# Decoder step: order of the operand splits at the entry of the gate-up product, a room of its own for one quarter, and the gate rows' loads on another queue

## The reference

```python
xp = xp + g1 * mix_out(o, bg * cy, attn_out_g[l], conv_out_g[l], w_o[l])        # output projection, residual
xp = xp + g2 * swiglu(modulate(xp, ln2_g[l], sh2, sc2), w_gu[l], w_down[l])     # the same for xs, with its own gates

def modulate(x, g, shift, scale):
    return rmsnorm(x, g) * (1.0 + scale) + shift

def swiglu(h, w_gu, w_down):
    g, u = jnp.split(h @ w_gu, 2, axis=-1)
    return (jax.nn.silu(g) * u) @ w_down
```

## Time and profile before

| | us |
|---|---|
| median of 3 runs | 961.69 (961.57 to 964.09) |
| profiled execution | 954.09 |
| its span, first to last instruction | 952.3 |
| TensorE busy | 911.9 |
| VectorE busy | 636.5 |
| ScalarE busy | 406.6 |
| GpSimd busy | 294.8 |

### The profile page before, as it was taken

How to read it: one execution, slowest core, us unless ns; L and a number is a source line. 1 busy time by engine, 2 the same in 40 slices (tenths; PEclk the granted TensorE clock), 3 DMA queues, 4 the chain that set the end, 5 groups by cost and what they waited for, 6 DMA issues and landing times.

```text
span 952.3 us, 16418 instructions
## 1 busy us (share of the span) xinstructions
PE 911.9 (96%) x6253; PEld 761.1 (80%) x6253; DVE 636.5 (67%) x1238; ACT 406.6 (43%) x818; POOL 294.8 (31%) x289
## 2 busy tenths in 40 slices
PE   6999999999999999899999988989999999999997
PEld 5777888999985557666644578989999999888886
DVE  3565773698646777667433879999998888544444
ACT  3674552221344335766601654444444445333220
POOL 4111000000132441534300347867767774000000
PEclk9999999999999999999999999999999999999999
DMA  8998313264449885473104232533333333522101
GB/s 274 397 393 294 106 50 97 81 208 150 148 140 350 321 320 190 130 257 89 35 1 132 85 104 64 148 89 89 90 89 90 105 110 107 200 89 89 72 1 50
DMA packets 84075, 138.83 MB, mean 146 GB/s; under 512 B 4259, under 2 KB 55027, under 8 KB 79646
## 3 DMA queue, kind: packets, MB, share of 16 engines
q1 hardware_dynamic: 74146, 95.47, 30.7%
q0 software_dynamic: 9568, 42.18, 12.5%
q10 hardware_dynamic: 284, 0.13, 0.0%
HBM read 130.58 MB, written 11.31 MB: 149 GB/s over the span
## 4 chain that ended last, share of the span: by engine, by line
PE 77%; DVE 9%; DMA 5%; issue 3%; ACT 3%; POOL 2%; SPq 0%; DVEq 0%; ACTq 0%; POOLq 0%
PE bank L2299 16%; PE bank L2301 16%; PE bank L2300 16%; PE bank L2293 6%; PE bank L2379 3%; PE bank L2813 3%; PE bank L2823 3%; DMA wring<-in_w_ada 2%; PE bank L2660 2%; PE bank L2630 2%; PE bank L2328 2%; PE bank L2793 2%; DMA arena<-in_cache_k_slc,idh 2%; PE bank L2309 2%; PE bank L2308 2%
## 5 line engine op out<-in xcount | busy, mean ns | idle before, releaser
L2299 PE MATMUL bank<-s,ring_hi 128*128 128x288 f32 x620 | 185.9, 300 | 10.5 <-DVE s L521 7.1
L2300 PE MATMUL bank<-s,ring_lo 128*128 128x288 f32 x620 | 184.5, 298 | 0.0
L2301 PE MATMUL bank<-s,ring_hi 128*128 128x288 f32 x620 | 183.8, 296 | 0.0
L2299 PEld LDWEIGHTS bank<-s,ring_hi 128*128 128x128 f32 x620 | 117.7, 190 | 11.5 <-DVE s L521 7.6
L2301 PEld LDWEIGHTS bank<-s,ring_hi 128*128 128x128 f32 x620 | 118.2, 191 | 0.0
L2300 PEld LDWEIGHTS bank<-s,ring_lo 128*128 128x128 f32 x620 | 117.8, 190 | 0.0
L521 DVE TENSOR_TENSOR ring_lo<-mem,ring_hi 128x512 fp32r<-128x512 f32 x84 | 107.6, 1300 | 0.0
L2293 PE MATMUL bank<-cst,arena 128*128 128x128 f32 (+1 forms) x538 | 69.1, 280 | 10.1 <-DMA arena<-in_cache_k_cmp,idx 6.5
L2293 PEld LDWEIGHTS bank<-cst,arena 128*128 128x128 f32 (+1 forms) x538 | 59.5, 143 | 23.8 <-issue 15.5
L886 POOL DMA_INDIRECT arena<-in_cache_k_slc,idh x16 | 15.4, 964 | 171.3 <-PE bank L2301 165.7
L521 DVE TENSOR_TENSOR dn_w<-wring,dn_w 128x2048 fp32r<-128x2048 f32 (+1 forms) x11 | 23.1, 2096 | 65.8 <-ACT dn_w L518 65.8
(11 more groups left out here) (363 smaller groups left out, 2099.0 us busy)
## 6 DMA issues: line engine op xcount, KB each, us to landing
wring<-in_w_gu SPq DMA_DIRECT2D x44, 512.0 KB, 5.1
wring<-in_w_ada SPq DMA_DIRECT2D x16, 1024.0 KB, 12.6
wring<-in_w_in SPq DMA_DIRECT2D x10, 1024.0 KB, 5.0
wring<-in_w_down SPq DMA_DIRECT2D x10, 1024.0 KB, 5.0
wring<-in_w_ada SPq DMA_DIRECT2D x16, 512.0 KB, 8.9
proj<-in_x_prompt SPq DMA_DIRECT2D x4, 512.0 KB, 12.2
mem<-in_state_k_win POOLq DMA_DIRECT2D x8, 256.0 KB, 8.6
mem<-in_state_v_win POOLq DMA_DIRECT2D x8, 256.0 KB, 6.0
```

The lines of the kernel that those rows point to most:

```text
L2299: pe.matmul(dst, sh, ml, start=first and k == 0, stop=False)
L2300: pe.matmul(dst, sl, mh, start=False, stop=False)
L2301: ins = pe.matmul(dst, sh, mh, start=False, stop=last and k == len(pairs) - 1)
```

## The change

Five edits, all around the entry of the gate-up product.

1. DVE does the last tile's modulation (L2168, L2170 before) right behind the low parts of (1,4) and slot 5. The low parts (0,7), (1,8) and (0,6), which stood ahead of it, come later: (1,8) right behind it, (0,7) ahead of (1,7), (0,6) ahead of (1,6). (2,8) and (2,4) come ahead of the first sum of the last segment. `SEG_LOW`, `SEG_HIGH` and ACT's list are put in that order.
2. POOL's `sums(1)` waits for the low part (2,4).
3. Operand 8 gets rooms of its own (`units[8]`): the high part in `arena`, where tiles 0 and 1 of the residual stood, the low part in `uvT`, which the output projection reads until its end. So ACT waits with (0,8) until the stores of those two tiles have landed (`x1_first_out`), and DVE does the low part of (0,8) behind the last of the projection.
4. Operand 3 then no longer waits for `plain_step(3)` on ACT. Its three high parts move ahead of slots 8 to 11 and its three low parts ahead of slot 9, from a place ahead of slot 12.
5. The four loads of the gate rows move from POOL's product loop to SP, behind the last tile's store, with a semaphore of their own.

```diff
-        units[8] = units[3]
+        units[8] = (arena, 2 * 1024), (uvT, 4 * HALF)
@@ sp
             x1_store(4)
+            sp.wait_ge(x1_ready, 10)
+            for y in range(2):
+                at0, cols = (2 + y) * 32 * 512, slice(512 * y, 512 * y + 512)
+                sp.dma_start(gbc[:, 0, cols], bass.AP(g_rows.tensor, at0, [[0, 128], [1, 512]])).then_inc(gates_back, 16)
+                sp.dma_start(gbc[0:TS, 1, cols], bass.AP(g_rows.tensor, at0 + 512, [[512, NB], [0, NQ], [1, 512]])
+                             ).then_inc(gates_back, 16)
             for i in range(g0 + 4, d0 + 4):
                 load(i)
@@ pool
             sums(0)
+            pool.wait_ge(seg_low, SEG_LOW.index((2, 4)) + 1)
             sums(1)
...
-                if p == 24:
-                    pool.wait_ge(x1_ready, 10)
-                    gates_load(1)
@@ act
-                if m == 3:
-                    want_filled(act, ("gp", 3))
...
                 if t == 3:
+                    act.wait_ge(x1_first_out, 32)
                     sums_high(0, 8)
...
             plain_silu(0, c11s[0])
-            sums_high(1, 5)
             sums_high(2, 8)
             sums_high(2, 4)
             slot_cast(6)
+            first_copy(1)
+            sums_high(1, 5)
             sums_high(1, 7)
-            first_copy(1)
...
             plain_silu(2, c21)
+            for s in range(3):
+                sums_high(s, 3)
             slot_cast(8)
             slot_cast(9)
             first_copy(2)
             slot_cast(10)
             slot_cast(11)
-            for s in range(3):
-                sums_high(s, 3)
@@ dve
+                    if n and t == 5:
+                        sums_low(0, 8)
...
                             sums_low(0, 4)
-                            sums_low(0, 8)
                             slot_rest(4)
...
             slot_rest(5)
-            sums_low(0, 7)
-            sums_low(1, 8)
-            sums_low(0, 6)
             key = ("hT", 4, 0)
...
-            dve.tensor_tensor(s_raw[5][:, :, seg], a21, a22, ALU.add).then_inc(seg_last, 1)
+            sums_low(1, 8)
             sums_low(2, 8)
             sums_low(2, 4)
+            dve.tensor_tensor(s_raw[5][:, :, seg], a21, a22, ALU.add).then_inc(seg_last, 1)
...
+            sums_low(0, 7)
             sums_low(1, 7)
...
             sums_low(2, 7)
-            sums_low(1, 6)
-            sums_low(2, 6)
+            for s in range(3):
+                sums_low(s, 6)
             slot_rest(8)
+            for s in range(3):
+                sums_low(s, 3)
             plain_product(3, c21, actT[:, 0, HALF:TOK])
...
             slot_rest(11)
-            for s in range(3):
-                sums_low(s, 3)
             slot_rest(12)
```

More of the change, by code:

```diff
@@ L74 @@
 SEGS = ((2, 0, 96), (3, 96, 224), (4, 224, 288))
-SEG_HIGH = [(0, 4), (0, 8), (0, 5), (0, 7), (0, 6), (1, 4), (1, 8), (1, 5), (2, 8), (2, 4), (1, 7), (2, 5), (1, 6), (2, 7), (2, 6),
+SEG_HIGH = [(0, 4), (0, 8), (0, 5), (0, 7), (0, 6), (1, 4), (1, 8), (2, 8), (2, 4), (1, 5), (1, 7), (2, 5), (1, 6), (2, 7), (2, 6),
             (0, 3), (1, 3), (2, 3)]
-SEG_LOW = [(0, 4), (0, 8), (0, 5), (1, 4), (0, 7), (1, 8), (0, 6), (2, 8), (2, 4), (1, 5), (1, 7), (2, 5), (2, 7), (1, 6), (2, 6),
+SEG_LOW = [(0, 4), (0, 5), (0, 8), (1, 4), (1, 8), (2, 8), (2, 4), (1, 5), (0, 7), (1, 7), (2, 5), (2, 7), (0, 6), (1, 6), (2, 6),
            (0, 3), (1, 3), (2, 3)]
@@ L441, in decoder_kernel @@
         win_loaded = [sem(f"win_loaded{i}") for i in range(2)]
-        gates_out, gates_in = sem("gates_out"), sem("gates_in")
+        gates_out, gates_in, gates_back = sem("gates_out"), sem("gates_in"), sem("gates_back")
         xin_loaded, rows_back, rows_out, stored, kvc_stored = (
             sem(n) for n in ("xin_loaded", "rows_back", "rows_out", "stored", "kvc_stored"))
-        x1_out, x1_back, slot_high, slot_low, made, seg_sum, seg_last, seg_high, seg_low, first_silu, second_silu, t_made, c22_made, gu_done = (
-            sem(n) for n in ("x1_out", "x1_back", "slot_high", "slot_low", "made", "seg_sum", "seg_last", "seg_high", "seg_low",
+        x1_out, x1_first_out, x1_back, slot_high, slot_low, made, seg_sum, seg_last, seg_high, seg_low, first_silu, second_silu, t_made, c22_made, gu_done = (
+            sem(n) for n in ("x1_out", "x1_first_out", "x1_back", "slot_high", "slot_low", "made", "seg_sum", "seg_last", "seg_high", "seg_low",
                              "first_silu", "second_silu", "t_made", "c22_made", "gu_done"))
@@ L818, in x1_store @@
                 sp.wait_ge(x1_ready, 5 + t + 1)
-                sp.dma_start(x1_rows[128 * t:128 * t + TM[t], :], xin[t][0:TM[t], :]).then_inc(x1_out, 16)
+                sp.dma_start(x1_rows[128 * t:128 * t + TM[t], :], xin[t][0:TM[t], :]).then_inc(x1_first_out if t < 2 else x1_out, 16)
             for i in range(done + 14, g0 + 2):
@@ L827, in _ @@
             x1_store(4)
+            sp.wait_ge(x1_ready, 10)
[4 more added lines that the diff above has]
+                             ).then_inc(gates_back, 16)
             for i in range(g0 + 4, d0 + 4):
                 load(i)
-            sp.wait_ge(x1_out, 80)
+            sp.wait_ge(x1_first_out, 32)
+            sp.wait_ge(x1_out, 48)
             want_filled(sp, ("gu",) + FAST[-1])
@@ L1423, in _ @@
             slot_cast(6)
+            first_copy(1)
+            sums_high(1, 5)
             sums_high(1, 7)
-            first_copy(1)
             sums_high(2, 5)
+            slot_cast(7)
             sums_high(1, 6)
-            slot_cast(7)
             sums_high(2, 7)
@@ L2248, in _ @@
                     if f == 3:
-                        dve.wait_ge(x1_out, 80)
+                        dve.wait_ge(x1_first_out, 32)
+                        dve.wait_ge(x1_out, 48)
                     dve.tensor_tensor(actT[:, f, 0:HALF], c11s[f % 3], t_sum, ALU.mult).then_inc(gu_done, 1)
@@ L2259, in _ @@
                 low_job(j)
-            dve.wait_ge(gates_in, 128)
+            dve.wait_ge(gates_back, 64)
             dve.wait_ge(x1_back, 80)
```

## The result

The changed kernel takes 955.21 us (median of 7 runs, 950.59 to 957.63), the kernel before 961.76 (7 runs). The ratio is 0.9924, 95% interval 0.9896 to 0.9953: faster by 0.76%. The forecast was 959.5, no change that a measurement can tell. Its range held the time, but the likeliest case, no change, was the wrong one.

The account below looks back on a forecast made before the run. TensorE, busy 911.9 of 952.3 us, bounds the kernel; only about 13.2 us of stalls and clock drops can return. Entry +0.4 and gate rows -2.6 sum to -2.2: 959.5 us, own range 957.5 to 961.5, wider range 954.5 to 963.5.

Parts of the forecast that it names:

- The first stall: Ahead of plain_step(2): earlier modulation makes the stall zero, 4.48 + 1.3 us back for now.
- What the cover was: Ahead of (2,2): POOL's eight operations without a hole delay slot 7; TensorE waits 4.8 us, the first gain given back whole.
- The second stall: Ahead of (3,2): slot 9 late, 3.0 us wait and a clock drop; together with the stalls before it +0.4 us.
- The third stall: From (1,7) on: the 0.76 us stall is unchanged, 0, between -0.8 and +1.3 us.
- The gate rows: Last stall, near 619: without four transfers POOL is 2.4 us ahead and the pile-up goes, -2.6 us (0 to -2.7).
- The rule weighed: Shared SBUF ports: whichever starts first holds them; DVE waits out one POOL operation at a time, sum unchanged.
- that DVE keeps its lead: Rival at the entry: slots 7 and 9 in time, -13.2 us, 948.5; half-way some -6, 955.7; 17%.
- a variant without the second drop: Inside the forecast's case: no second clock drop, at (3,2), giving 958.1.
- No turn was lost further on: Rival at slots 15 to 18: DVE loses two turns plus a clock drop, +1.7 us, 963.4; 15%.
- four signs of being wrong: Slot 7 well before 567; POOL idle between slots 12 and 10; TensorE idle under 5 us, 554 to 584; stall near 619.
- The carried median: Whole kernel: runs' median lies 7.6 us above the profiled execution, so 951.9 becomes 959.5.

Follow-up runs that it names:

- e3: Changed kernel without POOL's wait for the low part (2,4) ahead of sums(1); 948.44 us, ratio 0.9900.
- g1: f1 with the plain product and slot 9's low part moved ahead of operand 3's low parts; 950.73 us, ratio 0.9887.
- g2: e3 with the plain product, which reads a PSUM bank, moved ahead of slot 8's low part; 953.38 us, ratio 0.9919.
- changed, again: The changed kernel once more, no edit; 955.50 us, ratio 0.9922.
- e2: Changed kernel with the four gate-row loads back on POOL; 955.81 us, ratio 0.9985.
- e3 again: e3 once more, no edit, beside f1 on one chip; 950.01 us, ratio 0.9878.
- f1: Changed kernel with POOL's wait for (2,4) moved from ahead of sums(1) to behind it; 948.73 us, ratio 0.9864.
- f1 again: f1 once more, no edit, beside e3 on one chip; 949.35 us, ratio 0.9869.
- f2: f1 with operand 3's parts one by one behind slots 10, 11, 12, and slot 9 ahead of the plain product; 951.92 us, ratio 0.9898.
- e4: Changed kernel with operand 3's high and low parts back behind slot 11, ahead of slot 12; 950.77 us, ratio 0.9923.
- e5: Changed kernel with the plain product between operand 3's first and second low part; one run, 954.09 us, no interval.
- e1: Kernel before with only the four gate-row loads moved from POOL to SP; 953.74 us, ratio 0.9956.

## Why the prediction was wrong

**The first stall.** Right: TensorE does not wait ahead of `plain_step(2)`.

**What the cover was.** Right, in time and size. Shifted by the 3.16 us, the forecast has POOL's last end at 569.7 and slot 7's low part at 570.3, with a wait of 4.8. Measured: 569.79, 570.34, 4.66. The gain of the first edit was given back whole, and e3 shows why: the wait of edit 2 made the chain.

**The second stall.** This is the step that failed: "`make` (2,5) holds the second until 571.8 + 0.55 = 572.35; `make` (2,6), freed by (3,1) at 572.2, holds the third until 573.5 + 0.28 = 573.8." I had carried the strict turns, read from a POOL with work queued, over to a POOL operation that starts from a wait. Measured in its place: neither held a part; DVE did all three in 1.49 us, the stall was 0.91 (0.25 in the second profile) in place of 3.0, and no clock drop followed it. Against the 2.65 + 1.3 of before this is a gain of 3.0 us where I had a loss of 0.4. These 3.4 us are the difference between the two sums, 3.2, but for what the other stalls differ by. g1 and g2 show that the operation that reads a bank decides here: moved, it moves `make`'s end, and both lengths were foretold. The ten profiles with `make` (2,5) ahead of or among DVE's subtractions, and one row of before:

| kernel | POOL starts | DVE's bank read starts | POOL ends | ends behind the read |
|---|---|---|---|---|
| changed | 573.50 | 574.71 | 575.93 | 1.22 |
| changed, again | 577.79 | 578.72 | 579.94 | 1.22 |
| e2 | 570.92 | 571.85 | 573.06 | 1.21 |
| e3 | 563.86 | 565.96 | 567.18 | 1.22 |
| e3 again | 567.61 | 569.71 | 570.94 | 1.23 |
| f1 | 570.81 | 573.65 | 574.87 | 1.22 |
| f1 again | 565.98 | 568.82 | 570.04 | 1.22 |
| f2 | 564.06 | 566.09 | 567.32 | 1.23 |
| g1 | 564.18 | 565.61 | 566.84 | 1.23 |
| g2 | 566.59 | 566.68 | 567.90 | 1.22 |
| before, a later slot | 606.28 | 606.83 | 608.05 | 1.22 |

The last line was there to be read before the forecast. DVE had a single operation under way there, so it could not tell "waits for the one that runs" from "waits for all up to the bank read"; but it is a row of a `make` that comes back from a hole, and I had looked at none. In e4 and e5, which are not in the table, `make` (2,5) came back while the bank read ran and took 1.28 us. In every row of the table what let POOL in was a bank read; whether another DVE operation with one operand in SBUF would do the same, no run here shows.

It is no rule for every wait. In five other rows POOL came back after a shorter hole, beside the low parts of slots 10 to 13, and got in ahead of DVE's next subtraction with no bank read between: in the changed kernel and its second profile, in e2, e4 and e5. The first and the fourth of them:

```profile
578.54 1.41 POOL L970 TENSOR_TENSOR mem<-wring 128x512 f32<-128x512 f32 x1 [0.90 <-PE bank L2306]
```

```profile
575.10 1.70 POOL L968 TENSOR_TENSOR mem<-wring,mem 128x512 f32<-128x512 f32 x1 [0.96 <-PE bank L2306]
```

The holes were 0.73 to 1.75 us there and 3.7 us or more in the first ten rows of the table. Whether the hole's length makes the difference, or that a DVE operation one or two earlier had itself waited for POOL, no run separates; nor do the profiles say why a POOL operation queued behind another gets every second turn. That stays open.

**The third stall.** Right: 0.86 against 0.76, within the bounds. In e5 it was 1.31, so it does depend on what goes on ahead of it.

**The gate rows.** Right: 2.62 us forecast as 2.6, and e1 gives 2.84 alone. That the drop behind it might come back (e2) was not in the sum; here it does not matter, since the stall is gone.

**The rule weighed.** The Trainium skill (SBUF — State Buffer, "SBUF: two separate sides") has the pair of ports go to whoever starts first, for the whole instruction. I let the sum go by it, and read into it that the one that waits comes next. Where POOL had work queued, its timeline agrees with that, 1.4 to 1.8 us from one start to the next. Behind the long hole it does not: in f1, `make` started at 570.81, and slot 8's part and operand 3's three began after that and were done first. The measurement decides. Either way DVE and POOL do not meet only at semaphores, as the opening has it of the engines.

**The rivals.** The one nearest to what happened was the first, that DVE keeps its lead. It held for operand 3's parts and not for slot 7. Its half-way value of -6 (955.7) lies near the -5.4 of the account and the median of 955.21, but that is luck: its condition, slot 7 by 564, was missed by 3.2 us. I gave the rival 17%, because I priced it as one state of affairs for the whole entry, when each place has its own. Inside the forecast's own case I had a variant without the second drop, 958.1; it was the right direction and too small by the stall itself. No turn was lost further on.

**The signs.** None of the four signs of being wrong came: TensorE stood idle for 5.6 us at the place where less than 5 was the sign. What told was the missing sign of being right, a wait near 3 us ahead of (3,2) with clock 0.50 behind it.

**The carried median.** The forecast put the median 7.6 us above the profiled execution, as it was before. After, it lay 3.3 us above (955.21 against 951.92). Of the fourteen traces, that of the kernel before is the only one in which TensorE has no half clock between its start and the entry. So 959.5 lies 4.3 us above the measured median. That the forecast of 951.9 for the profiled execution matched 951.92 is luck: the 3.16 us of the untouched part hid the 3.2 us by which the sum was short. The account is free of both.

## What to carry to other kernels

A price read beside an engine that always has work queued need not hold for the first operation after a wait: look for rows of that kind by themselves, with their bracket of idle time, before you multiply. When a wait is added to an engine that has slack, follow its whole chain; here the wait on POOL cost 3.3 us, and without it the change is worth 8.6 us of account in place of 5.4. And when profiles of two kernels are compared, anchor them at the last row of the part that was not touched: the spans agreed with the forecast to 0.1 us here and meant nothing.

## What the hardware showed that I had not expected

- `make` (2,5), behind 3.7 to 8.1 us of idle time, ended 1.21 to 1.23 us behind the start of DVE's next bank read in all ten profiles, however long DVE's row of subtractions ahead of it was; in f1 that made 4.06 us out of 1.3.
- The granted clock behind a stall of the same length differs: behind 2.62 us near 621 it was 1.00 before, behind 2.63 us at the same slot 0.62 in e2. In the fourteen profiles of the table, from the entry on, no stall of up to 1.85 us was followed by half clock that wasn't there before it, and every one of 3.43 us and more was.
- That does not hold for the part ahead of the entry, which is the same in both kernels. In the changed kernel's profile the clock was 0.50 near 250 us, behind stalls of 1.05 and 0.31 us, and near 393 us, behind one of 1.64; before, at stalls of the same length (1.05 and 0.32, 1.63), it stayed at 1.00. Thirteen of the fourteen profiles have such stretches, at changing places, and they move all that follows.
